# One block for heads, compression, scores and selection; an earlier last split and earlier rows in the expert passes

## The reference

```python
def compress_blocks(x, pe, w1, w2):          # x: (b, g, s, d), blocks of 32 rows every 16
    chunks = x.reshape(b, g, s // CMP_STRIDE, CMP_STRIDE, d)
    blocks = jnp.concatenate([chunks[:, :, :-1], chunks[:, :, 1:]], axis=3) + pe
    return jax.nn.gelu(blocks.reshape(b, g, n, CMP_BLOCK * d) @ w1) @ w2
q = rms_norm(q, q_norm_g)                    # per head; ks and kw the same with their gains
k_cmp = rms_norm(compress_blocks(kc, ...), k_norm_g[0]); v_cmp = compress_blocks(vc, ...)
sc = einsum('bgrqd,bgnd->bgrqn', q, k_cmp) * scale - slopes * dist_cmp
p_cmp = masked_softmax(sc, dist_cmp >= 0); o_cmp = einsum('bgrqn,bgnd->bgrqd', p_cmp, v_cmp)
imp = einsum('bgrqn,nj->bgqj', p_cmp, overlap)          # + 1e3 where forced
_, sel_idx = lax.top_k(imp, top_n)                      # 8 of 16 key blocks for each query
# experts: y[token] += gate * ((silu(x @ w_gate[e]) * (x @ w_up[e])) @ w_down[e])
```

## Time and profile before

| what | us |
|---|---|
| runs | 2114.24, 2118.39, 2119.51 |
| profiled execution | 2113.19 |
| its span | 2111.5 |
| TensorE busy | 1817.7 (86%) |
| VectorE busy | 1223.1 (58%) |
| ScalarE busy | 865.3 (41%) |
| GpSimd busy | 316.9 (15%) |

### The profile page before, as it was taken

One profiled execution on the slowest core, in us unless ns is written; L12 is line 12 of the kernel. 1 busy time (PEld: TensorE's weight loads), 2 busy tenths in 40 slices (PEclk: granted clock), 3 DMA queues, 4 the chain that ended last, 5 costly groups with the idle time before them and its releaser, 6 DMA issues. The chain is left out here.

```text
span 2111.5 us, 25605 instructions
## 1 busy us (share of the span) xinstructions
PE 1817.7 (86%) x9608; PEld 1505.6 (71%) x9608; DVE 1223.1 (58%) x1566; ACT 865.3 (41%) x928; POOL 316.9 (15%) x258
## 2 busy tenths in 40 slices
PE   8999998376898999949999982999999949999980
PEld 7888887364677788837888761888887847888760
DVE  5323333755645445558999866332325557999973
ACT  4102222312333342227888863211102127888860
POOL 0000000101000001122434310000000122343410
PEclk9999999867899999969999995999999969999995
DMA  5333332602000024277999948211206258999947
GB/s 204 130 116 125 102 126 86 135 1 80 1 1 1 1 82 157 90 292 273 376 378 370 373 191 289 78 40 50 68 32 218 100 232 317 380 383 372 377 160 309
DMA packets 145297, 374.40 MB, mean 177 GB/s; under 512 B 40078, under 2 KB 75150, under 8 KB 120446
## 3 DMA queue, kind: packets, MB, share of 16 engines
q1 hardware_dynamic: 113542, 309.54, 39.9%
q0 software_dynamic: 22432, 45.53, 6.0%
q10 hardware_dynamic: 9216, 17.93, 2.2%
HBM read 331.38 MB, written 75.10 MB: 193 GB/s over the span
## 5 line engine op out<-in xcount | busy, mean ns | idle before, releaser
L1253 PE MATMUL ex_ps_h<-odd_split 128*128 128x512 f32 x768 | 196.1, 406 | 8.1 <-DVE odd_split L1367 7.9
L1253 PE MATMUL ex_ps_h<-even_split 128*128 128x512 f32 x768 | 195.1, 405 | 8.3 <-DVE even_split L1367 8.0
L1253 PEld LDWEIGHTS ex_ps_h<-odd_split 128*128 128x128 f32 x768 | 142.4, 192 | 47.5 <-DVE odd_split L1367 14.4
L1253 PEld LDWEIGHTS ex_ps_h<-even_split 128*128 128x128 f32 x768 | 142.0, 191 | 47.4 <-DVE even_split L1367 14.3
L517 PE MATMUL in_ps<-in_w_hi,in_xT_hi 128*128 128x512 f32 (+1 forms) x448 | 172.1, 384 | 1.7 <-DVE in_xT_lo L422 1.7
L517 PE MATMUL in_ps<-in_w_lo,in_xT_hi 128*128 128x512 f32 (+1 forms) x448 | 169.0, 377 | 0.0
L517 PE MATMUL in_ps<-in_w_hi,in_xT_lo 128*128 128x512 f32 (+1 forms) x448 | 168.9, 377 | 0.0
L1640 PE MATMUL conv_ps<-conv_xT_hi,conv_w_hi 128*128 128x512 f32 x384 | 150.5, 392 | 0.9 <-DVE conv_w_lo L1578 0.9
L1640 PE MATMUL conv_ps<-conv_xT_lo,conv_w_hi 128*128 128x512 f32 x384 | 149.9, 390 | 0.0
L1640 PE MATMUL conv_ps<-conv_xT_hi,conv_w_lo 128*128 128x512 f32 x384 | 149.9, 390 | 0.0
L2349 ACT ACTIVATE att_prob<-att_ps_s 128x512 f32<-128x512 f32 x114 | 68.0, 597 | 175.0 <-PE att_ps_s L2287 174.8
(11 more groups left out here) (343 smaller groups left out, 3981.4 us busy)
## 6 DMA issues: line engine op xcount, KB each, us to landing
all_region<-in_moe_w_gate SPq DMA_DIRECT2D x16, 1024.0 KB
all_region<-in_moe_w_up SPq DMA_DIRECT2D x16, 1024.0 KB
all_region<-in_moe_w_down SPq DMA_DIRECT2D x16, 1024.0 KB
experts_w_gu<-in_moe_w_gate SPq DMA_DIRECT2D x16, 1024.0 KB
experts_w_gu<-in_moe_w_up SPq DMA_DIRECT2D x16, 1024.0 KB
experts_w_d<-in_moe_w_down SPq DMA_DIRECT2D x16, 1024.0 KB, 15.6
all_region<-in_ev_w_in SPq DMA_DIRECT2D x12, 1024.0 KB, 8.2
proj<-in_stage ACTq DMA_DIRECT2D x48, 256.0 KB, 2.1
```

What stands on the lines that cost most here:

```text
L1253: last = pe.matmul(ps_h[:, u % 2, :], a[:, u % 2, k, :], w[:, k, :], start=(k == 0 and j == 0), stop=(k == KT - 1 and j == 2))
```

## The change

Edit A puts `rows_of_heads` and the three blocks of `sparse_prepare` into one block, `prepare_attention`. The doubled copy on GpSimd is gone; TensorE makes both halves with plain products of the raw rows (64 columns of weights) by the identity, in four groups through one PSUM place. The gains of the keys are applied when the transposed heads are taken, as a scale for each partition, and their loads come as single elements. The sum of exponentials comes from the activation's accumulator, with one activation for each head and tile, and the negative maximum is its bias. The head sum is two additions. Scores, selection and the gated output are interleaved by batch; the score places in PSUM are two instead of four batches.

Edit B concerns `experts`. The last expert's down piece is split into the place of the first half of gate and up; SP loads the stream's tiles as soon as experts 28 and 29 have left `region`; GpSimd reads the fullest expert's count at the start of its list. The diff, cut to its core:

```diff
@@ class Split
+    def last_down(self):
+        return [self.part(j * KT * 2 * DE, DE // P, D) for j in range(2)]
@@ experts, sync
-                waves(sp, wave, first=1)
-                sp.wait_ge(finished, 1)
-                following.load(sp)
+                for piece in (SECOND, DOWN):
+                    sp.wait_ge(piece_lo[piece], NE - B + 1)
+                following.load(sp, range(NT - 2))
+                for e in range(2):
+                    sp.wait_ge(x_turned[e], NE // B)
+                following.load(sp, range(NT - 2, NT))
...
+                later_waves(sp, fullest(sp), wave, landed, load_again)
@@ experts, gpsimd
+                full = fullest(pool)
...
-                waves(pool, wave, first=1)
+                later_waves(pool, full, wave, landed)
@@ experts, scalar
+                def high_last(n, u):
+                    act.wait_ge(down_loaded[u % B], 16 * uses(n, u) + 16)
+                    act.wait_ge(piece_used[FIRST], n * U + (u + 1))
+                    act.activation(last_down[0], data.raw(DOWN, u % B), ACT.Copy).then_inc(piece_hi[DOWN], 1)
...
                     if following:
                         high(*following, FIRST)
+                    else:
+                        high_last(*this)
                     gate(*this)
...
                     rows_out(*last)
-                    high(*this, DOWN)
+                    if following:
+                        high(*this, DOWN)
@@ prepare_attention, sync
+                sp.dma_start(q_rows[:], con["q_rows"]...).then_inc(rows_ext_loaded, 16)
+                sp.dma_start(kvc[:, 0, :, :], tiled[:, :, C_KC:C_VC]).then_inc(kvc_loaded[0], 16)
+                sp.dma_start(gains[:, 0:1], q_gain.rearrange("(d b) -> d b", b=1), ...).then_inc(gains_loaded, 16)
+                sp.dma_start(gains[:, 1:4], k_gains.rearrange("b d -> d b"), ...).then_inc(gains_loaded, 16)
...
@@ prepare_attention, scalar
-                    act.activation(keep.kT[0:HD, :, :, t * P:(t + 1) * P],
-                                   ps_n[0:HD, 2, :, :].rearrange("p (b g) n -> p b g n", b=2), ACT.Copy).then_inc(k_taken, 1)
+                    for b in range(2):
+                        last = act.activation(keep.kT[0:HD, b, :, t * P:(t + 1) * P], ps_n[0:HD, 2, b * G:(b + 1) * G, :],
+                                              ACT.Copy, scale=gains[:, 2 + b:3 + b])
+                def exps(b):
+                    act.wait_ge(maxima, b + 1)
+                    if b >= 2:
+                        act.wait_ge(p_turned, (b - 1) * BATCH)
+                        act.wait_ge(selected, b - 1)
+                    for t in range(BATCH):
+                        for h in range(NH):
+                            i = (b * BATCH + t) * NH + h
+                            last = act.activation(pc[:, b % 2, t, h, :], ps_s[b % 2][:, t, h, :], ACT.Exp,
+                                                  bias=less[:, i:i + 1], accum_out=total[:, i:i + 1])
+                    last.then_inc(exped, 1)
...
+                    if t == 4:
+                        hidden(0)
+                        hidden(1)
@@ prepare_attention, vector
                 for t in range(NT):
                     if t + 2 < NT:
                         sums(t + 2)
                     if t + 1 < NT:
                         apply(t + 1)
+                    if t == 1:
+                        add_places(0, 1)
+                    if t == 2:
+                        add_places(1, 1)
+                    if t == 6:
+                        norm_compressed()
                     take(t)
+                    if t < 2:
+                        add_places(t, 0)
+                    if t == 5:
+                        sum_compressed()
+                    if t == 6:
+                        take_compressed()
...
+                maximum(0)
+                maximum(1)
+                for b in range(BATCHES):
+                    select(b)
+                    if b + 2 < BATCHES:
+                        maximum(b + 2)
+                    if b:
+                        open_gates(b - 1)
+                open_gates(BATCHES - 1)
@@ prepare_attention, tensor
+                def turn_rows(j, g):
+                    pe_.wait_ge(kvc_loaded[j], 16)
+                    pe_.wait_ge(xb_ready, j * G + g)
+                    for t in range(NT):
+                        for a in range(2):
+                            last = pe_.matmul(ps_x[a * HD:(a + 1) * HD, t * P:(t + 1) * P], kvc[:, j, t, g * HD:(g + 1) * HD],
+                                              cst.ident[:], start=True, stop=True)
+                    last.then_inc(x_turned, 1)
...
+                for t in range(NT):
+                    turn_heads(t)
+                    if t == 0:
+                        turn_rows(0, 0)
+                    if t == 1:
+                        turn_rows(0, 1)
+                        turn_rows(1, 0)
+                    if t == 2:
+                        turn_rows(1, 1)
+                        hide(0)
+                    if t == 3:
+                        hide(1)
+                    if t == 5:
+                        compress()
+                    if t == 6:
+                        turn_compressed()
...
+                score(0)
+                score(1)
+                for b in range(BATCHES):
+                    if b + 2 < BATCHES:
+                        score(b + 2)
+                    weigh(b)
```

More of the change, by code:

```diff
@@ L1232, in wave, with landed @@
                     rest(w)
-                waves(pool, wave, first=1)
+                def landed():
+                    for t in range(NT - 2, NT):
+                        pool.wait_ge(following.loaded[t], 16)
+                later_waves(pool, full, wave, landed)
             @block.tensor
@@ L1293, in end @@
                     turn_h(*last)
-                    down(*last)
+                    down(*last, *last_down)
                 rounds(pe, start, step, end)
@@ L1401, in step @@
                         low(*following, SECOND)
-                    low(*this, DOWN)
+                        low(*this, DOWN)
                 dve.memset(data.later_rows, 0.0).then_inc(zeroed, 1)
@@ new lines, in prepare_attention @@
+        peT = m.sb("peT", [P, 2, L])
+        w1s = m.sb("w1s", [P, 2, L, CMP_HID])
+        w2s = m.sb("w2s", [P, 2, HD])
+        hid = m.sb("hid", [P, 2, G, 2, NC_])
+        kc = m.sb("kc", [NC_, G, HD])
+        ksq = m.sb("ksq", [NC_, G, HD])
+        kss = m.sb("kss", [NC_, G])
+        pc = m.sb("pc", [P, 2, BATCH, NH, NC_])
+        less, total = (m.sb(n, [P, NT * NH]) for n in ("less", "total"))
+        hs_2 = m.sb("hs_2", [P, BATCH * G, 2, NC_])
+        hs = m.sb("hs", [P, BATCH * G, NC_])
@@ L1721, in rows_of_heads @@
+        p_turned, pT_ready, o_done, o_taken, g_exp = (
+            m.sem(n) for n in ("p_turned", "pT_ready", "o_done", "o_taken", "g_exp"))
         tiled = proj.rearrange("(t p) n -> p t n", p=P)
-        with nc.Block() as block:
+        with nc.Block(no_gpsimd_drain=True) as block:
             @block.sync
@@ L1754, in _ @@
                     pool.wait_ge(mask_loaded, 16 * (j + 1))
-                    pool.tensor_copy(keep.masks[:, at], masks_f[:])
-                    pool.drain()
-                pool.wait_ge(pool_loaded, 32)
-                for j in range(2):
-                    for a in range(2):
-                        pool.tensor_copy(keep.kvc2[:, j, :, :, a, :], kvc[:, j, :, :].rearrange("p t (g d) -> p t g d", d=HD))
+                    last = pool.tensor_copy(keep.masks[:, at], masks_f[:])
+                    if j == 0:
+                        pool.drain()
+                last.then_inc(masks_ready, 1)
                 pool.drain()
@@ new lines, in sum_compressed, with norm_compressed, take_compressed @@
+                def sum_compressed():
+                    dve.wait_ge(k_sq, 1)
+                    dve.tensor_reduce(kss[:], ksq[:], X, ALU.add).then_inc(k_sum, 1)
+                def norm_compressed():
+                    dve.wait_ge(k_root, 1)
+                    dve.reciprocal(kss[:], kss[:])
+                    dve.drain()
+                    dve.tensor_tensor(kc[:], ps_k, kss[:].unsqueeze(2).to_broadcast([NC_, G, HD]), ALU.mult).then_inc(k_ready, 1)
+                def take_compressed():
+                    dve.wait_ge(v_done, 1)
+                    for a in range(2):
+                        rows = slice(a * HD, (a + 1) * HD)
+                        dve.tensor_copy(keep.v_cmp[rows, :, a * HD:(a + 1) * HD], ps_v[rows, :, :])
+                    dve.wait_ge(k_turned, 1)
+                    dve.tensor_scalar(keep.kcT[0:HD, :, :], ps_t, gains[:, 1:2], None, ALU.mult).then_inc(compressed, 1)
@@ L2092, in sparse_prepare @@
-        with Pool_(nc, name + "S2") as b2:
-            pT = b2.sb("pT", [P, 2, NH // 2, P])
-            ps_p = b2.ps("ps_p", [P, 2, NH // 2, P])
-            ps_o = b2.ps("ps_o", [P, 2, NSA_W])
```

(39 more changed lines are left out.)

488 lines of the change are left out of this document (215 added, 273 removed).

## The result

The changed kernel takes 2056.45 us (median of 4 runs, 2054.59 to 2058.54) against 2118.95 (4 runs, 2114.24 to 2119.59): ratio 0.971, 95% interval 0.9691 to 0.9729. It is 62.5 us faster. The profiled execution took 2058.26 (span 2056.7), 54.9 us less than before; the forecast for it was 2068.8.

A forecast was written before the change was run, and what follows sets the result against it. It saw a chain of four barrier-separated stages (365 to 505.3) and latency at pass ends as bounds; 22 + 22.4 = 44.4 us off 2113.2 gave 2068.8, named 2074 since the median lay 5.2 higher; range 2060 to 2092.

The forecast's parts named there:

- Start of the block: Loads ahead of the merged block's first compute: first turn at about 379.7, 0.6 us later; element loads taken as 0.
- Raw rows: Plain products of raw rows in the merged block: four groups in series, each 3.7 us at the upper clock level.
- The rival that I listed on this term: Raw-row products cost four turns each: groups of 7.7 us, part A gives 6, total 2090; chance 0.03.
- Additions, stall: VectorE's additions after each raw-row group take 2.5 us; it idles 5.8 us for the squares; scores start 3.5 us earlier.
- Scores to gated output: End of the merged block, 69.4 us before: 51 us, between 44.5 (upper clock level) and 56 (lower).
- rival (1): Scores run at the upper clock level throughout: part A gives 28.5 us, total 2067; chance 0.12.
- Part A: Merged block of heads, compression, scores and selection: gives 22 us, from 15 to 28.
- Part B: Ends of both expert passes: 11.2 us a pass, 22.4 for both, from 7 to 26.
- Rival (2): Pass end wins only the 3.6 us of earlier start; part B gives 7, total 2089; chance 0.12.
- (4): TensorE stays at the lower clock level through the merged block, ending 18 us later: total 2114, no change; chance 0.04.
- (5): ScalarE's 64 small exponentials set the merged block's end; at 1.5 us each 39 us late, total 2135; chance 0.03.

The follow-up runs named there:

- e3: Changed kernel with raw-row products reordered, all eight tiles into partitions 0 to 63, then all into 64 to 127; 2066.2 us, ratio 0.9767.
- e6: Changed kernel with the last expert's down piece split late, as before; early row loads and early count kept; 2069.46 us, ratio 0.9800.
- e8: Changed kernel with idle transpositions on TensorE in the pauses around the scores; 2053.94 us, ratio 0.9724.
- e9: The changed kernel itself run once more, to see the spread of its block; 2056.34 us, ratio 0.9716.
- e13: Changed kernel with Gelu one tile later, two wide products among each tile's scores and idle transpositions in the pauses; 2050.4 us, ratio 0.969.
- e5: Changed kernel with the stream's row loads and the count read late, as before; early split of the down piece kept; 2070.25 us, ratio 0.9804.

## Why the forecast missed, step by step

The miss of 17.5 us has two parts: 10.5 in the profiled execution (2068.8 forecast, 2058.3 measured), and 7.0 because I added 5.2 us for the distance of the median from the profiled execution, while the changed kernel's median lies 1.8 under its own. That addition was no mechanism. The medians of the kernel before were 2112.9 to 2119.0 on the chips of this case, so a single profiled execution gives the total within some 5 us and no better. That medians put 37.7 us on the block where traces put 29 to 33 I can't explain; which stage of the kernel before is slower in its other executions stays open.

Point by point:

- **Start of the block**: forecast 379.7 for the first turn, measured 379.17. The element loads were hidden, as taken.
- **Raw rows: the step that failed.** "a group of 16 costs 3.7 us at the upper level" was 1.97 (2.83 for the first, partly at the lower one, 4.2 forecast). I took the price from a row of 128-column weights and let it stand for 64-column ones that go to different halves in turn; they overlap. Four groups on the chain make 1.4 + 3 x 1.75 = 6.7 us. e3 shows it: apart, the later groups take 3.30, and the scores start 5.6 us later. The rival that I listed on this term (7.7 us, four turns each) lay on the wrong side, and nothing below 3.7 was in its bounds.
- **Additions, stall**: pairs of 2.44 us (2.5) and 5.48 us of stall (5.8) came as forecast. Scores start 11.0 us earlier than before, not 3.5; 6.7 of the 7.5 missing are the groups, the start gives 0.5.
- **Scores to gated output**: forecast 51 between 44.5 and 56, measured 47.4. The exponentials cost 0.29 each, not 0.40: 1.7 us less ahead of the first selection. The clock was at the upper level for tiles 0 to 3, at the lower one from 431.5 to 445.2 (tiles 4 and 5 and the products behind them), and at the upper for tiles 6 and 7; rival (1), the upper level throughout, did not come true either. I put the 3.6 us down to these two, but that is argued, and their shares can't be parted, as the clock alone moves this stretch by 5 us. I had also given TensorE 13.3 us a batch at the lower level, where my own terms (7.3 and 5.8) make 13.1; the bound of 56 barely changes.
- **Part A** so gave 33.0 instead of 22, with bounds of 15 to 28: the upper bound missed the overlap.
- **Part B** gave 21.6 for 22.4. Earlier start 3.7 (3.6), faster product 2.4 (2.6), scatter and rows 4.1 to 5.2 with the count (5.0). That the sum came out within 0.8 us is in part luck: taken back alone, the rows cost 5.4 to 5.7 (4.0) and the count 0.5 to 0.7 (1.0), and in the second pass these overlap with the split's 6.7. Rival (2), that only the earlier start is won, is refuted: e6, without an earlier start, has pass ends 6.1 and 3.6 us shorter than before.
- **Rivals (4) and (5)**: the clock was up for most of the merged block, and the small exponentials were cheap; both fell.

## What to carry to other kernels

Before pricing a product on TensorE, look where its outputs go: two products with 64 columns of weights into different halves of the partitions, issued one after the other, cost together little more than one (1.97 against 3.30 us for 16), and swapping two loops loses it. Loads that the next stage needs are best moved into a lull ahead of a latency chain: beside the last scatter they cost 5.4 to 5.7 us with the early split, and moving them (with the early count) gave 3.6 and 6.1 us without it. Parts of an edit that meet on one chain should be taken out one by one and also put in one by one, since the two give different sizes. Bound a new shape from below as well as from above, and don't move a forecast by the distance between one profiled execution and a median.

## What the hardware showed that I had not expected

- TensorE's granted clock fell from its upper to its lower level (1.2 GHz) while TensorE was at work: in e8 at 425.6, in e9 at 425.5 and in e13 at 422.7, 2.3 to 3.8 us after a last pause of 1.1 us, and it stayed down for 14 to 20 us of nearly unbroken work. The same instructions then differ by 5 us between traces.
- Products of 64-column weights into alternating halves of the partitions overlap: single records start 0.055 us apart on average, against 0.109 us when neighbours write the same half (e3).
- Reading the accumulator after an activation of 64 columns costs 0.08 us of pace (0.29 against 0.21), since the read of 0.19 us overlaps the next start.
- A scatter of 128 rows landed in 3.6 us alone, in 7.4 us when 4.2 MB of loads had begun 7.2 us before it (kernel before), and in 8.6 us when they had begun 3.9 us before it (e5).
